# A four-part edit of a decoder trunk on one core: softmax rows scaled on GpSimd, outputs split straight from PSUM, pooling cut in pieces, another order ahead of attention

## The reference, cut to what matters

```python
x = x + 0.5 * swiglu(rms_norm(x, g1), gate1, up1, down1)
z = rms_norm(x, gm) @ w_in          # q, k, v (8 heads x 64), indexer, pooled channels, memory queries
y_attn = dsa_attention(q, k, v, ...)      # 8 heads; each query keeps its top 128 admissible keys
y_pool = multiscale_pool(pu) @ w_pool     # trailing windows 2/4/8/16, minus the token
y_mem  = memory_attention(mq, mem)        # 4 heads over 256 memory tokens
x = x + concat([y_attn, y_pool, y_mem]) @ w_out
x = x + 0.5 * swiglu(rms_norm(x, g2), gate2, up2, down2)
```

## Time and profile before

| what | value |
|---|---|
| time before, median of 3 runs | 1943.56 us (1941.02 to 1945.83) |
| profiled execution: its own time / its span | 1942.63 us / 1940.8 us |
| TensorE busy | 1908.7 us, 98% |
| ScalarE busy | 958.7 us, 49% |
| VectorE busy | 623.0 us, 32% |
| GpSimd busy | 348.4 us, 18% |
| granted TensorE clock, mean | 0.996 |

### The profile page before, as it was taken

How to read it: one execution, slowest core, us unless ns; L and a number is a source line. 1 busy time by engine, 2 the same in 40 slices (tenths; PEclk the granted TensorE clock), 3 DMA queues, 4 the chain that set the end, 5 groups by cost and what they waited for, 6 DMA issues and landing times.

```text
span 1940.8 us, 25996 instructions
## 1 busy us (share of the span) xinstructions
PE 1908.7 (98%) x9100; PEld 1549.0 (80%) x9100; DVE 623.0 (32%) x1181; ACT 958.7 (49%) x1294; POOL 348.4 (18%) x397
## 2 busy tenths in 40 slices
PE   7999999999899999999999999999998999999999
PEld 6888888887668888888888888888875688888887
DVE  5222200377753322210052222004777442222101
ACT  5444443565565544443364444336656564444432
POOL 1111111112411111111111111111225011111110
PEclk9999999999999999999999999999998999999999
DMA  7888888878137888888878888888780379888885
GB/s 221 211 191 196 189 194 194 191 180 208 42 88 173 206 195 190 197 186 202 190 184 194 195 192 194 195 185 208 175 205 6 87 184 221 191 195 191 196 191 140
DMA packets 96105, 348.15 MB, mean 179 GB/s; under 512 B 10800, under 2 KB 11056, under 8 KB 95792
## 3 DMA queue, kind: packets, MB, share of 16 engines
q0 software_dynamic: 46512, 169.37, 49.3%
q1 hardware_dynamic: 48960, 175.67, 27.8%
q10 hardware_dynamic: 576, 2.36, 0.3%
HBM read 175.91 MB, written 2.10 MB: 92 GB/s over the span
## 4 chain that ended last, share of the span: by engine, by line
PE 94%; DVE 2%; issue 1%; ACT 1%; DMA 1%; SPq 0%; DVEq 0%; ACTq 0%; POOLq 0%
PE bank L507 93%; PE bank L863 1%; DMA w_lo<-raw 1%; DVE h_lo L1186 0%; DMA raw<-weights 0%; DVE x L1209 0%; DVE z L1366 0%; DVE t L1414 0%; DVE pt L358 0%; DVE sq L1192 0%; ACT prob L1125 0%; DVE mk_n L1372 0%; ACT t L1125 0%; ACT a_hi L1141 0%; ACT a_hi L1112 0%
## 5 line engine op out<-in xcount | busy, mean ns | idle before, releaser
L970 ACT ACTIVATE w_hi<-raw 128x1024 fp32r<-128x1024 f32 x323 | 342.1, 1059 | 831.9 <-PE bank L507 794.9
L507 PE MATMUL bank<-h_hi,w_hi 128*128 128x512 f32 x1648 | 647.4, 393 | 9.2 <-ACT h_hi L949 8.3
L507 PE MATMUL bank<-h_hi,w_lo 128*128 128x512 f32 x1648 | 642.6, 390 | 0.0
L507 PE MATMUL bank<-h_lo,w_hi 128*128 128x512 f32 x1648 | 627.3, 389 | 0.1
L418 POOL DMA_DIRECT2D w_lo<-raw x323 | 278.3, 867 | 1498.3 <-ACT w_lo L971 1461.4
L507 PEld LDWEIGHTS bank<-h_hi,w_hi 128*128 128x128 f32 x1648 | 310.2, 188 | 80.6 <-issue 14.1
L507 PEld LDWEIGHTS bank<-h_hi,w_lo 128*128 128x128 f32 x1648 | 310.2, 188 | 65.0
L507 PEld LDWEIGHTS bank<-h_lo,w_hi 128*128 128x128 f32 x1648 | 309.6, 188 | 65.6 <-issue 1.4
L971 ACT ACTIVATE w_lo<-raw 128x1024 fp32r<-128x1024 f32 x323 | 336.6, 1042 | 0.0
L507 PE MATMUL bank<-a_hi,w_hi 128*128 (+1 forms) x832 | 324.6, 390 | 0.0
L507 PE MATMUL bank<-a_lo,w_hi 128*128 (+1 forms) x832 | 323.8, 389 | 0.0
(11 more groups left out here) (149 smaller groups left out, 1145.4 us busy)
## 6 DMA issues: line engine op xcount, KB each, us to landing
raw<-weights SPq DMA_DIRECT2D x326, 512.0 KB, 4.7
w_lo<-raw POOLq DMA_DIRECT2D x323, 512.0 KB, 6.0
x<-x_t SPq DMA_DIRECT2D x4, 512.0 KB, 7.2
mem<-mem_t ACTq DMA_DIRECT2D x2, 1024.0 KB, 6.7
out_t<-x SPq DMA_DIRECT2D x8, 256.0 KB, 2.1
const<-consts SPq DMA_DIRECT2D x1, 481.5 KB, 10.0
wpool<-pool_w ACTq DMA_DIRECT2D x2, 128.0 KB, 6.8
par<-params SPq DMA_DIRECT2D x1, 38.0 KB, 3.3
```

What stands on the lines that cost most here:

```text
L507: return nc.tensor.matmul(out_, lhsT, rhs, start=start, stop=stop, skip_group_check=True)
L970: nc.scalar.activation(w_hi[:, s], raw[:, s], ACT.Copy).then_inc(w_hi_done, 1)
```

## The change

1. The exponentials are scaled before they are transposed: VectorE inverts the sums of each pair of units, GpSimd multiplies the two probability tiles by them in place. `spread_sums`, `copy_rt` and `over_sums` go, and with them `rt` and `yt`; the outputs are split from their PSUM bank. Transposes wait for `scaled_ready`. The lag grows from 4 to 6 units, with six probability tiles in place of four. One more bank (7) is filled early.
2. GpSimd's pooling is cut in seven pieces that stand behind the scaling of pairs 4, 6, 7, 9, 10, 12 and 13, and the DMAs of the first four `out` slots behind pairs 5, 6, 11 and 12. The one-operation multiply in it gets a second multiply by 1.0. The pooling maps stand at steps 24 and 34.
3. Ahead of attention VectorE makes one round earlier and the last two rounds behind the evacuation of the memory queries and the normalised keys; ScalarE's second square of the memory queries stands ahead of the splits of the keys; TensorE makes their sums in the middle of the first pooled projection (behind 5 of its 8 chunks).
4. In the very first FFN `token_sums` stands between slots 2 and 3.

```diff
-POOL_UNITS = (30, 32)
+POOL_UNITS = (24, 34)
-LAG = 4
+LAG = 6
+PROBS = 6
+OUT_REST_PAIRS = (5, 6, 11, 12)
+POOL_PAIRS = (4, 6, 7, 9, 10, 12, 13)
-FILL = {UNITS - 2: (0,), UNITS: (1,), UNITS + 2: (4,), UNITS + LAG: (2, 3)}
+FILL = {UNITS - 2: (7,), UNITS: (0,), UNITS + 2: (1,), UNITS + 4: (4,), UNITS + LAG: (2, 3)}
...
+            def less_mean(l, i, half):
...
                 step(l, G.tensor_scalar(w[p, 16:T], w[p, 16:T],
-                                        const[p, C_INVW + i:C_INVW + i + 1], None, ALU.mult))
+                                        const[p, C_INVW + i:C_INVW + i + 1], 1.0, ALU.mult, ALU.mult))
                 step(l, G.tensor_tensor(out=ui[p, :], in0=w[p, :], in1=ui[p, :], op=ALU.subtract))
+            def pooling(l, at_pair):
+                if at_pair in POOL_PAIRS:
+                    pool.wait_ge(scaled_ready, l * UNITS + 2 * at_pair + 2)
+                if at_pair == 4:
+                    wait_apart(pool, proj_ready, l * PROJ + PROJ)
+                    shifted_sum(l, 0, wa, chunk(u, 0), 1)
+                    shifted_sum(l, HD, wb, wa, 2)
+                elif at_pair == 6:
+                    less_mean(l, 0, 0)
+                elif at_pair == 7:
+                    less_mean(l, 0, 1)
+                elif at_pair == 9:
+                    shifted_sum(l, 0, wa, chunk(u, 1), 1)
+                    shifted_sum(l, 0, wb, wa, 2)
+                elif at_pair == 10:
+                    shifted_sum(l, 0, wa, wb, 4)
+                    shifted_sum(l, HD, wb, wa, 8)
+                elif at_pair == 12:
+                    less_mean(l, 1, 0)
+                elif at_pair == 13:
+                    less_mean(l, 1, 1)
+            def scale_pair(l, m):
+                pool.wait_ge(rinv_ready, l * (UNITS // 2) + (m + 1))
+                for n in (2 * m, 2 * m + 1):
+                    p = prob[n % PROBS][:, 0:unit(n)[3] * P]
+                    G.tensor_scalar(p, p, rinv[:, n:n + 1], 1.0, ALU.mult,
+                                    ALU.mult).then_inc(scaled_ready, 1)
...
-                pooling(l)
-                rests(l, ahead, SLOTS if l == LAYERS - 1 else SLOTS + BEGUN)
+                for m in range(UNITS // 2):
+                    scale_pair(l, m)
+                    pooling(l, m)
+                    if m in OUT_REST_PAIRS:
+                        rest(l, ahead + OUT_REST_PAIRS.index(m))
+                rests(l, ahead + RING, SLOTS if l == LAYERS - 1 else SLOTS + BEGUN)
...
-                token_sums(l, ph)
-                gate_up(0, 1)
+                if l == 0 and e == 0:
+                    gate_up(0, 1, token_sums)
+                else:
+                    token_sums(l, ph)
+                    gate_up(0, 1)
...
-                project_z(14, "pu", 0)
+                pool_slot(range(0, 5))
                 heads_sum(2)
+                pool_slot(range(5, DC))
...
-                    pe.wait_ge(p_ready, l * UNITS + (n + 1))
+                    pe.wait_ge(scaled_ready, l * UNITS + (n + 1))
...
-                        pe.wait_ge(y_ready, l * 2 * TT + (g - 1))
-                    if h == 0 and g > pools_after and is_mem:
-                        pe.wait_ge(ypool_lo, (l + 1) * 2)
+                        pe.wait_ge(yt_lo, l * 2 * TT + (g - 1))
...
-                    if n - 2 in group_after:
-                        spread_sums(group_after[n - 2])
...
                 square(2 * QT)
+                square(2 * QT + 1)
                 for j in range(QT, 2 * QT):
                     act.wait_ge(zn_ready, l * QT + (j - QT + 1))
                     act.wait_ge(zlo_ready, l * ZT + (j - QT + 1))
                     split_hi(j)
-                square(2 * QT + 1)
...
-                    if n >= 4:
-                        act.wait_ge(ptp_done, l * UNITS + (n - 3))
+                    if n >= PROBS:
+                        act.wait_ge(ptp_done, l * UNITS + (n - PROBS + 1))
...
                 inverse_columns(0)
+                rounds(1)
                 dve.wait_ge(hrms_ready, l * ROOT_GROUPS + 2)
...
-                rounds(1)
                 evacuate_z(2 * QT)
-                dve.wait_ge(gain_ready, l + 1)
-                for s in range(QT):
-                    dve.wait_ge(spread_done, l * QT + (s + 1))
-                    t = chunk(z, QT + s)
-                    V.scalar_tensor_tensor(out=t, in0=t, scalar=gain_qk[:, 0:1], in1=bank[4 + s][:, :],
-                                           op0=ALU.mult, op1=ALU.mult).then_inc(zn_ready, 1)
                 dve.wait_ge(mk_rms_ready, l + 1)
...
-                rounds(1)
                 evacuate_z(2 * QT + 1)
-                rounds(1)
+                dve.wait_ge(gain_ready, l + 1)
+                for s in range(QT):
+                    dve.wait_ge(spread_done, l * QT + (s + 1))
+                    t = chunk(z, QT + s)
+                    V.scalar_tensor_tensor(out=t, in0=t, scalar=gain_qk[:, 0:1], in1=bank[4 + s][:, :],
+                                           op0=ALU.mult, op1=ALU.mult).then_inc(zn_ready, 1)
+                rounds(2)
...
-                def invert_sums(g):
-                    units = slice(group_start(g), group_end(g))
-                    dve.wait_ge(p_ready, l * UNITS + group_end(g))
-                    V.reciprocal(rinv[:, units], rowsum[:, units]).then_inc(rinv_ready, 1)
+                def invert_sums(n):
+                    dve.wait_ge(p_ready, l * UNITS + n)
+                    V.reciprocal(rinv[:, n - 2:n], rowsum[:, n - 2:n]).then_inc(rinv_ready, 1)
-                    V.tensor_tensor(out=yt[:, 0:c], in0=y_bank(g)[:, 0:c], in1=rt[:, 0:c],
-                                    op=ALU.mult).then_inc(y_ready, 1)
...
-                    V.tensor_tensor(out=lo, in0=yt[:, 0:n * P].rearrange("p (c t) -> p c t", t=P),
+                    V.tensor_tensor(out=lo, in0=y_bank(g)[:, 0:n * P].rearrange("p (c t) -> p c t", t=P),
                                     in1=hi.bitcast(f32), op=ALU.subtract).then_inc(yt_lo, 1)
```

More of the change, by code:

```diff
@@ L196, in build @@
     prob = [t1[:, 0:T], t1[:, T:2 * T]] + \
-           [place(f"prob{i}", T, h_at + (4 + i) * tile_b)[:, :] for i in range(2)]
-    rt = place("rt", T, h_at + 6 * tile_b)
-    yt = place("yt", T, h_at + 7 * tile_b)
+           [place(f"prob{i}", T, h_at + (4 + i) * tile_b)[:, :] for i in range(PROBS - 2)]
     squares = [t1[:, 0:T], t1[:, T:2 * T], t2[:, 0:T], t2[:, T:2 * T]]
@@ new lines, in shifted_sum @@
+            def shifted_sum(l, p0, dst, src, by):
+                G.tensor_tensor(out=dst[p0:P, by:T], in0=src[p0:P, by:T],
+                                in1=src[p0:P, 0:T - by], op=ALU.add)
+                step(l, G.tensor_copy(dst[p0:P, 0:by], src[p0:P, 0:by]))
+            def less_mean(l, i, half):
+                ui, w = chunk(u, i), (wa, wb)[half]
+                p = slice(half * HD, (half + 1) * HD)
+                G.tensor_tensor(out=w[p, 0:16], in0=w[p, 0:16],
+                                in1=const[p, C_INV + 16 * i:C_INV + 16 * (i + 1)], op=ALU.mult)
+                step(l, G.tensor_scalar(w[p, 16:T], w[p, 16:T],
+                                        const[p, C_INVW + i:C_INVW + i + 1], 1.0, ALU.mult, ALU.mult))
+                step(l, G.tensor_tensor(out=ui[p, :], in0=w[p, :], in1=ui[p, :], op=ALU.subtract))
+                if half:
+                    pool.sem_inc(pooled_ready, 1)
@@ L593, in gate_up @@
                     for up in range(2):
+                        if up and between:
+                            between(l, ph)
                         pos = place_of(l, n + up)
@@ L729, in project_z, with pool_slot @@
                     project(l, at(name, i), bank[t % 4][:, :], h_hi, h_lo)
+                def pool_slot(ks):
+                    n = at("pu", 0)
+                    for k in ks:
+                        last = passes(bank[2][:, :], weight(place_of(l, n), k * P),
+                                      pair(h_hi, h_lo, k * T), k == 0, k == DC - 1)
+                    if ks[-1] == DC - 1:
+                        last.then_inc(slot_done, 1)
                 def project_kv(s):
```

102 lines of the change are left out of this document (25 added, 77 removed).

## The result

The changed kernel takes **1961.69 us** (median of 4 runs, 1956.44 to 1964.49) against 1942.78 (4 runs) for the kernel before on the same chip: a ratio of 1.0087, interval 1.0072 to 1.0102. It is 19 us slower where I forecast 11 us faster. The profiled execution is the fastest of the four, 1956.44 us with a span of 1954.6; before, the span was 1940.8. So the trace has 13.8 of the 19 us.

A forecast was written before the change was run, and what follows sets the result against it. The prediction took TensorE, 94% of the chain, as the bound. Start +3.4, ahead of attention -7.4, clock -1.3 and attention -5.6 made -10.9 us on 1942.6: 1931.7, predicted as a 1932.5 us median, range 1919 to 1952.

The forecast's parts named there:

- may also lower the clock: TensorE pauses of 5 us or more, at 34 us or step 34: one to three us more, kept in the range.
- GpSimd's queue on the path: Attention: scaling, pooling and DMA issues take 31.6 us from pair 4, so TensorE stands 5.9 us at step 34.
- The rate: GpSimd's scaling in attention: two-operation multiply at the cast's 1.37 ns a column, 0.7 us for 512 columns.
- Rival 3: GpSimd's scaling in attention keeps 3.07 ns a column: +11.1 us a layer, 1960 us in all; chance 0.13.
- Attention without waits: Attention without any wait for GpSimd: 72.5 us less 6.1 of spreads and 2.6 of idle time, 63.8 us.
- rival 1: Attention: GpSimd keeps up and TensorE never waits, -8.7 us a layer, 1921 us in all; chance 0.22.
- The start: First FFN: later token sums delay slot 4's rounding and DMA, so TensorE waits for it: +3.4 us.
- rival 4: First FFN: TensorE doesn't wait for slot 4's DMA, start term -1.9, 1927 us; chance 0.07 with the forecast's rate.
- Ahead of attention: Before attention in each layer: VectorE's reordered work fills its pauses, attention begins 3.7 us sooner, -7.4 us for both.
- -1.3 us for a better clock: Layer 1 ahead of attention: the pause splits into two under 2 us, the clock stays at its upper level: -1.3 us.
- The early fill of bank 7: Attention: output work moved forward from behind, worth nothing.

The follow-up runs named there:

- c_spread: Changed kernel with the token sums back in their old place, pooling's first half ahead of pair 0, its second half spread, output slots' DMAs later: 1927.4 us.
- a_start_back: Changed kernel with only the token sums of the very first FFN back in their old place: 1951.39 us.
- experiment 12: c_spread with the probabilities scaled by a one-operation multiply, without the second multiply by 1.0: 1948.89 us.
- c_ramp: c_spread plus throwaway matmuls in TensorE's two pauses ahead of attention: 1922.27 us.
- experiment 6: c_spread with the first FFN's token sums between slots 2 and 3 again and slot 4 rounded ahead of ScalarE's root: 1929.79 us.
- Experiment 7: Kernel before with only the new order ahead of attention, plus throwaway matmuls in TensorE's two pauses there: 1931.22 us, against 1936.55 without them.
- experiment 11: c_ramp with the early fill of bank 7 taken back: 1921.62 us.
- b_pause: Kernel before, with TensorE made to wait for unused GpSimd additions ahead of the transposes of steps 32 and 34: 1950.62 us.
- b_pause3: Kernel before, with TensorE made to wait for more unused GpSimd additions, at steps 30, 32 and 34: 1972.2 us.
- a_pool_early: Changed kernel with the pooling of u's first half moved ahead of pair 0: 1948.84 us (12 runs, 1933.75 to 1957.47).

## Why the prediction was wrong

**The step that failed** is the sentence behind the rivals: that such a pause "may also lower the clock", for "one to three us more". I priced the clock by the example that I had read: 0.76 in the window around layer 1's pause of 4.46 us ahead of attention. There much of the slow stretch is hidden, since VectorE sets the end of it; what is seen is 10.34 us for attention's first piece where layer 0 has 8.90. Behind step 34 it is TensorE that sets the end, with 20 us of work ahead. The same sentence speaks of pauses of 5 us or more, and the sum took it that two pauses of under 2 us would keep the clock up; the longest in attention was 2.75 us. From runs: c_spread to the changed kernel is 34.3 us (1961.69 less 1927.4). Of that the start is 4.3. GpSimd's waits are 12.7 by the trace (6.6 and 6.1), less the 3.2 us by which c_spread waits longer for VectorE's masks (3.7 against 0.5): 9.5. What is left is **20.5 us, which I put to the clock**. It is a difference of medians, and two other readings bear it out: filling the two longest pauses of each layer gave 19.5 back, and by the windows (busy time times what the clock lacks) the low clock costs some 22 us in the changed kernel's profiled execution and 5 in c_spread's, 17 of the 29 us between these two, where the changed kernel's was the fastest of its four. The forecast held +5.9 a layer for the waiting and nothing for this. Had I counted it, the sum would have been -10.9 + 20 = +9, on the right side. Most of the rest up to +19 is attention without waits, 3 us a layer short, the stretch that no edit touches, 3.3, and the start, 0.9.

**GpSimd's queue on the path: right.** The forecast for the wait at step 34 was 5.9 us a layer; the five waits come to 6.6 and 6.1. The queue from pair 4 to the last piece was to take 31.6 us and took 33.1 (523.51 to 556.62). It began 17.8 us into attention, not 14.6. The slow clock of the first stretch explains most of that: the chain's first piece there is 9.86 us for 35 matmuls, and 7.29 for 34 in the trace of a_start_back, where the clock stood.

**The rate: right,** 1.36 ns a column for 1.37, and the reason too: the 3.07 ns row belongs to the form with the empty second operation, as experiment 12 shows. Rival 3's time, 1960 us, came true without its mechanism; a time that matches says nothing for a cause. I had put the advice of the Trainium skill, GPSIMD Engine Reference, section 4.1, on that rival's side; its factor of about 2 is given for work with two inputs, and this multiply has one. The Trainium skill, GPSIMD Engine Reference, section 3.1, gives 769 ns as the best case for 512 elements; the trace has 697, so here the measurement is the better number.

**Attention without waits: too hopeful.** c_ramp comes near it: keys aside, attention and output projection take 99.05 us in layer 0 (500.50 to 599.55) against 104.71, 5.7 us less, where rival 1 had 8.7. The spreads' 6.1 us are there; the 2.6 us of idle time are not. In c_ramp's 70 us from 500 TensorE is idle for 2.8. Waits of 1.22 and 0.64 us for VectorE's masks are there now in place of those that went; I had taken every wait in the windows for one that the change removes.

**The start: right in kind, short in size.** +3.4 was forecast and +4.3 came. The DMA was issued at 35.91 and not 35.0; its landing of 4.54 us is the one I had taken. My rival 4 assumed that a DMA alone holds slot 4; experiment 6 shows a second chain that holds it to 36.30 once the sums are late, no sooner than the 36.21 of before, and that I had not seen. The low clock behind that wait (1.5 us by the windows) wasn't in the sum either.

**Ahead of attention: right, the clock's share not.** -4.2 and -4.6 us for -3.7 each. Of the surplus 0.4 us in each layer is the selection mask, which became shorter; GpSimd's last split runs beside more of it before than after, but no run tests that. In layer 1 TensorE, then at its lower level, had also been ready 0.3 us later than VectorE. VectorE's mask before, then its normalisation of the memory keys and its mask after:

```profile
502.75 1.39 DVE L1383 TENSOR_SCALAR score<-score 128x1152 f32<-128x1152 f32 x1
```
```profile
490.63 0.76 DVE L1371 TENSOR_TENSOR mk_n<-kv,mk_rms 128x256 f32<-128x256 f32 x2
...
503.45 0.96 DVE L1387 TENSOR_SCALAR score<-score 128x1152 f32<-128x1152 f32 x1
```

The normalisation is shorter too, 0.76 us where it took 2.88, and GpSimd's splits no longer run beside it; it now stands ahead of the keys and so outside this stretch. The Trainium skill, SBUF - State Buffer, section "Who interferes with whom", has it that VectorE with two inputs in SBUF and GpSimd reading SBUF hold each other up; the trace agrees. So do the output splits: 0.69 us for 512 columns and 0.42 for 256 throughout, with one input in PSUM and GpSimd at work. The -1.3 us for a better clock did not come. The pause did not split into two: the 1.36 us one was there before, behind the 4.44 us one, and the 1.68 us one, for u, is new. Together they leave 0.72 in attention's first window in layer 0, and they stand right ahead of attention, where before the low stretch (500 to 504 us) was over when it began. Experiment 7 gives 5.3 us for filling them, with the reservation made there.

**The early fill of bank 7, "worth nothing":** the output projection now waits 0.48 and 1.51 us for slot 4's DMA, where it did not. These waits go in experiment 11, but its time couldn't tell what they cost.

## What to carry to other kernels

When a change gives TensorE new pauses, count each pause and then, as the bad case, up to some 25 us of work behind it at half speed, and look at the granted clock window by window, for the view of waits doesn't show it. Before a helper engine is put on the path, lay out its queue against the steps that need it: the same work in another order (with the start undone) was worth 34 us here. A gap that can't be closed may be worth filling with throwaway matmuls, where a bank is free and the fill is about as long as the gap.

## What the runs showed of the hardware

- Short pauses move the granted clock. One of 2.02 us, which ended at 557.46, was followed by the lower level to about 561 (b_pause: 0.80 in the window 555 to 560, 0.93 in 560 to 570); 0.69, 3.10 and 1.19 us within 13 us by 0.50 until 583, some 20 us behind the last (b_pause3); 1.22 and 0.64 us, 11 us apart, by nothing (c_spread). The same program can fall or not from one execution to the next: 24 us between the runs of a_pool_early. No run here says what exactly decides it.
- The clock also falls without such a pause. In the kernel before it is 0.66 from 404 to 409 us, where TensorE was idle for 0.32 us at the most; ahead of the fall it made 2 us of matmuls of 1x1 and 4x4 and a few of 64x256. The changed kernel has the same behind the same matmuls in layer 1 (1378 to 1382) and not in layer 0.
- GpSimd's multiply by a column takes 1.554 us for 128x512 with one operation and 0.697 with a second multiply by 1.0.

The windows of b_pause around and behind its pause:

```profile
555.00:560.00 5.00, 2.98 (x24) 2.09 (x23) 2.14 (x8) 2.21 (x7) 3.27 (x4) 0.80 0.93 305
560.00:570.00 10.00, 9.90 (x106) 7.39 (x106) 7.33 (x29) 6.95 (x27) 1.05 (x2) 0.93 0.07 28
```
